# Expert results of a mixture-of-experts layer: added to the residual on chip by a one-hot product, instead of stored and gathered

## The reference, cut to what matters

```python
e_flat = (g_sel[:, None] * EXPERTS_PER_GROUP + top_i).reshape(-1)   # two of 32 experts per token
...
def run_block(args):
    xb, e = args
    return (jax.nn.silu(xb @ w_eg[e]) * (xb @ w_eu[e])) @ w_ed[e]
...
out = jnp.zeros((T, D_MODEL), jnp.float32).at[t_buf].add(y_buf.astype(jnp.float32) * w_buf[:, None])
```

## Time and profile before

| | us |
|---|---|
| median of 3 runs (lowest, highest) | 1305.26 (1303.16, 1308.2) |
| the profiled execution, its own time | 1295.43 |
| the profiled execution, span from first to last instruction | 1293.6 |
| PE busy, all of the span | 1077.7 (83%) |
| DVE, ACT, POOL busy | 427.6, 365.0, 195.6 |

### The profile page before, as it was taken

How to read it: one execution, slowest core, us unless ns; L and a number is a source line. 1 busy time by engine, 2 the same in 40 slices (tenths; PEclk the granted TensorE clock), 3 DMA queues, 4 the chain that set the end, 5 groups by cost and what they waited for, 6 DMA issues and landing times.

```text
span 1293.6 us, 15640 instructions
## 1 busy us (share of the span) xinstructions
PE 1077.7 (83%) x6419; PEld 764.3 (59%) x6419; DVE 427.6 (33%) x736; ACT 365.0 (28%) x567; POOL 195.6 (15%) x207
## 2 busy tenths in 40 slices
PE   4899799999999999999999378887877877877830
PEld 4898677777989899999999333222322322322310
DVE  5122667653256555434323511111111111101115
ACT  5313567565566443434211100000000000000002
POOL 7000110111313365513100000000000000000012
PEclk9999899999999999999989588898988988988975
DMA  7555222231222121252630789999999999999934
GB/s 198 187 104 109 64 50 46 45 51 39 67 65 65 51 74 58 74 155 72 189 140 33 284 355 419 428 427 427 427 428 429 426 427 431 427 427 429 400 117 155
DMA packets 101179, 284.67 MB, mean 220 GB/s; under 512 B 4588, under 2 KB 77512, under 8 KB 88824
## 3 DMA queue, kind: packets, MB, share of 16 engines
q1 hardware_dynamic: 91392, 256.39, 53.8%
q0 software_dynamic: 5936, 19.69, 4.1%
q10 hardware_dynamic: 3784, 7.65, 1.7%
HBM read 262.96 MB, written 20.75 MB: 219 GB/s over the span
## 4 chain that ended last, share of the span: by engine, by line
PE 55%; DMA 27%; DVE 8%; ACT 5%; issue 4%; POOL 1%; SPq 1%; POOLq 0%; ACTq 0%; DVEq 0%
DMA arena<-in_w_expert_up 23%; PE za L1020 12%; PE pj L713 10%; PE pj L714 10%; PE pj L715 10%; DMA ring<-in_w_in 2%; PE pj L740 2%; PE zb L1035 2%; DVE arena L1579 1%; DVE arena L1578 1%; PE zb L838 1%; DMA arena<-yd,arena 1%; PE ms L996 1%; ACT arena L1218 1%; PE zb L836 1%
## 5 line engine op out<-in xcount | busy, mean ns | idle before, releaser
L1020 PE MATMUL za<-arena 128*64 128x512 f32 x1024 | 246.4, 638 | 61.5 <-DMA arena<-in_w_expert_up 47.2
L713 PE MATMUL pj<-u_high_r,ring_r 128*128 128x288 f32 x768 | 236.9, 309 | 8.4 <-DVE ring_r L1462 4.8
L714 PE MATMUL pj<-u_rest_r,ring_r 128*128 128x288 f32 x768 | 227.8, 297 | 0.0
L715 PE MATMUL pj<-u_high_r,ring_r 128*128 128x288 f32 x768 | 227.7, 296 | 0.0
L1020 PEld LDWEIGHTS za<-arena 128*64 128x64 f32 x1024 | 81.0, 147 | 216.1 <-issue 148.2
L713 PEld LDWEIGHTS pj<-u_high_r,ring_r 128*128 128x128 f32 x768 | 145.8, 190 | 16.5 <-issue 11.2
L714 PEld LDWEIGHTS pj<-u_rest_r,ring_r 128*128 128x128 f32 x768 | 145.8, 190 | 2.2 <-issue 1.0
L715 PEld LDWEIGHTS pj<-u_high_r,ring_r 128*128 128x128 f32 x768 | 145.6, 190 | 0.0
L1035 PE MATMUL zb<-arena 128*64 128x512 f32 x512 | 124.9, 644 | 17.3 <-DVE arena L1910 15.1
L1462 DVE TENSOR_TENSOR ring_r<-ring,ring_r 128x1024 fp32r<-128x1024 f32 x68 | 85.6, 1266 | 120.7 <-ACT ring_r L1106 120.6
L1035 PEld LDWEIGHTS zb<-arena 128*64 128x64 f32 x512 | 40.1, 147 | 91.1 <-issue 73.3
(11 more groups left out here) (408 smaller groups left out, 1699.6 us busy)
## 6 DMA issues: line engine op xcount, KB each, us to landing
arena<-in_w_expert_gate SPq DMA_DIRECT2D x32, 2048.0 KB, 20.7
arena<-in_w_expert_up SPq DMA_DIRECT2D x32, 2048.0 KB, 19.4
arena<-in_w_expert_down SPq DMA_DIRECT2D x32, 2048.0 KB, 19.8
ring<-in_w_in SPq DMA_DIRECT2D x32, 512.0 KB, 8.2
ring<-in_w_gate SPq DMA_DIRECT2D x24, 512.0 KB, 4.1
yd<-arena SPq DMA_DIRECT2D x16, 512.0 KB, 22.0
yd<-arena POOLq DMA_DIRECT2D x1, 4608.0 KB, 18.8
arena<-in_x_prompt SPq DMA_DIRECT2D x8, 512.0 KB, 7.2
```

The costliest lines, as they stand in the source:

```text
L713: pe.matmul(out, left[0], right[0], start=k == 0, stop=False)
L714: pe.matmul(out, left[0], right[1], start=False, stop=False)
L715: return pe.matmul(out, left[1], right[0], start=False, stop=k == last - 1)
L1020: m = pe.matmul(za[j * BLK:(j + 1) * BLK, b, :], xT[:, k, j * BLK:(j + 1) * BLK], w[:, j * KD + k, :], start=k == 0, stop=k == KD - 1)
```

## The change

The results of a pair no longer leave the chip. For each pair, DVE builds `slot_hot` (128 rows by 640 tokens), which is 1 where row r belongs to token t. ACT and DVE take the two halves of the down product out of `zb`, multiply each row by its weight, and split it into a rounded part `y_high` and a remainder `y_rest`, both in the fp32r form that PE multiplies in one pass. PE multiplies `slot_hot` with both (`scatter`): 2 halves by 5 token tiles are 10 chunks of two matmuls with 512 columns, which go in turn through four PSUM banks (the two of `pj` and the two of `zb`), and DVE adds each chunk to `h` (`add`). The chunks of pair i-1 are spread over pair i: six behind the first transposes, two behind up, two behind the transposes of `hid`. Those of pair 15 come behind the loop and behind the nine `If`s.

Per-row weights need a second table product (`col_weight`, 20 more matmuls), and pair 0 now waits for it (`routed` at 3). The copy to `hidT` moves from DVE to ACT. `store_y`, `yd`, the zero fill, the final gathers and `experts_done` go. The overflow pairs get their own path (`scatter_over`, `add_over`) in the bodies of the `If`s.

```diff
@@ SP
-                    store_y(i)
...
-            sp.wait_ge(S["y_out"], 16 * EPAIRS)
...
-            sp.sem_inc(S["experts_done"], 1)
@@ PE
+            def scatter(i, parts, behind=True):
+                for k in parts:
+                    q, t = divmod(k, NT)
+                    o0, n = TT[t]
+                    if k == 0:
+                        pe.wait_ge(S["hot_r"], i + 1)
+                        if behind:
+                            pe.wait_ge(S["sc_r"], 2 * NT * i)
+                    if k == 3:
+                        pe.wait_ge(S["yl_r"], 2 * i + 2)
+                    pe.wait_ge(S["yl_r"], 2 * i + q + 1)
+                    if k >= NBANK:
+                        pe.wait_ge(S["sc_r"], 2 * NT * i + k - NBANK + 1)
+                    bank = add_bank(k)
+                    half = slice(q * 512, (q + 1) * 512)
+                    pe.matmul(bank[0:n, :], slot_hot[:, o0:o0 + n], y_high[:, half], start=True, stop=False)
+                    pe.matmul(bank[0:n, :], slot_hot[:, o0:o0 + n], y_rest[:, half], start=False, stop=True
+                              ).then_inc(S["sc_ps"], 1)
...
             def expert_pair(i, turn, before=True, over=None, first=False):
+                else:
+                    pe.wait_ge(S["routed"], 3)
...
                 m.then_inc(S["xt2_ps"], 1)
+                if mix:
+                    scatter(i - 1, range(6), not first)
                 pe.wait_ge(S["xt2_a"], i + 1)
...
+                if mix:
+                    scatter(i - 1, (6, 7))
                 pe.wait_ge(S["hid_r"], i + 1)
...
                 m.then_inc(S["hidt_ps"], 1)
+                if mix:
+                    scatter(i - 1, (8, 9))
+                    pe.wait_ge(S["sc_r"], 2 * NT * (i - 1) + 8)
                 pe.wait_ge(S["hidt_r"], i + 1)
...
                 with pe.If(total > j):
-                    expert_pair(EPAIRS + j, ((EPAIRS + j) % 2, (EPAIRS + j) // 2))
+                    expert_pair(EPAIRS + j, ((EPAIRS + j) % 2, (EPAIRS + j) // 2), over=j)
+                    scatter_over(j)
+            scatter(EPAIRS - 1, range(2 * NT))
@@ DVE
+                dve.tensor_tensor(col_weight, bc(iota_f[:, 0:NPC].unsqueeze(1), P, k2, NPC),
+                                  bc(flat[1].unsqueeze(2), P, k2, NPC), ALU.is_equal)
...
+                dve.wait_ge(S["route_ps"], 3)
+                dve.tensor_copy(slot_weight, ms[:, P:P + NPC]).then_inc(S["routed"], 1)
...
+            def add(i, parts, behind=True):
+                for k in parts:
+                    q, t = divmod(k, NT)
...
+                    v = h[0:n, t, q * 512:(q + 1) * 512]
+                    dve.tensor_tensor(v, v, add_bank(k)[0:n, :], ALU.add).then_inc(S["sc_r"], 1)
...
+                    dve.tensor_scalar(slot_hot, tok_no, slot_tok[:, bass.ds(i, 1)], None, ALU.is_equal)
...
+                        dve.scalar_tensor_tensor(out=y_rest[:, half], in0=zb[:, q, :],
+                                                 scalar=weight_now, in1=y_high[:, half],
+                                                 op0=ALU.mult, op1=ALU.subtract).then_inc(S["yl_r"], 1)
...
+            add(EPAIRS - 1, range(NT))
             for t in range(NT):
-                final(t)
+                add(EPAIRS - 1, (NT + t,))
                 if t > 0:
                     final_norm(t - 1)
@@ POOL
-            pool.dma_start(yd[NE * BLK:(NE + OVB) * BLK, :].rearrange("(c p) d -> p c d", p=P),
...
-            pool.wait_ge(S["experts_done"], 1)
...
-                    pool.indirect_dma_start(out=y_back[t % 2][s][0:n, :], out_offset=None, in_=yd,
```

More of the change, by code:

```diff
@@ L251 @@
 NEARLY = 3
+NBANK = 4
 NMIX = 2 + NT
@@ L434, in trunk_and_experts @@
         iota_pf = at(u2T_off + D + OVB * NE + P, P)
-        g_ffn = at(take(D), D)
+        g_ffn_off = take(D)
+        g_ffn = at(g_ffn_off, D)
         lg = at(take(NT * 36), NT, 36)
@@ L454, in trunk_and_experts @@
         eid = at(take(OVB), OVB)
+        take(-cut[0] % 8)
+        slot_hot = region("slot_hot", take(NT * P), NT * P)
+        tok_no = at(take(NT * P), NT * P).bitcast(I32)
         cut[0] = merged_off
@@ L461, in trunk_and_experts @@
         hid = at(take(DE), DE)
-        y_out_sb = at(take(D), D)
+        y_off = take(D)
         w_g = [at(wexp_off, 2 * KD, DE), at(take(2 * KD * DE), 2 * KD, DE)]
         assert cut[0] <= front
-        y_back = [[at(wexp_off + D * (2 * i + s), D) for s in range(2)] for i in range(2)]
+        y_high = region("y_high", y_off, D)
+        y_rest = region("y_rest", g_ffn_off, D)
+        over_high = region("over_high", u2_off, D)
+        over_rest = region("over_rest", u2_off + D, D)
+        over_hot = region("over_hot", u2T_off + D, NT * P)
+        square = [at(wexp_off + 16384 + D * i, D) for i in range(2)]
+        col_weight = at(merged_off + D + 2 * NT * P + 2 * NT * NPC, 2 * NT, NPC)
         cs = [small]
@@ L998, in ffn_turn, with scatter_over, expert_pair @@
                 m.then_inc(S["lg_ps"], 1)
-            def expert_pair(i, turn, before=True):
+            def scatter(i, parts, behind=True):
[16 more added lines that the diff above has]
+                              ).then_inc(S["sc_ps"], 1)
+            def scatter_over(j):
+                for k in range(2 * NT):
+                    t, q = divmod(k, 2)
+                    o0, n = TT[t]
+                    if k == 0:
+                        pe.wait_ge(S["hot_r"], EPAIRS + j + 1)
+                    pe.wait_ge(S["yl_r"], 2 * (EPAIRS + j) + q + 1)
+                    if k < 2:
+                        pe.wait_ge(S["sc_r"], 2 * NT * (EPAIRS - 1))
+                    else:
+                        pe.wait_ge(S["over_r"], 2 * NT * j + k - 1)
+                    half = slice(q * 512, (q + 1) * 512)
+                    pe.matmul(pj[0:n, q, :], over_hot[:, o0:o0 + n], over_high[:, half], start=True, stop=False)
+                    pe.matmul(pj[0:n, q, :], over_hot[:, o0:o0 + n], over_rest[:, half], start=False, stop=True
+                              ).then_inc(S["over_ps"], 1)
+                pe.wait_ge(S["over_r"], 2 * NT * (j + 1))
+            def expert_pair(i, turn, before=True, over=None, first=False):
+                mix = before and over is None
                 pe.wait_ge(S["xg_in"], (i + 1) * 16)
@@ L1027, in expert_pair @@
                 m.then_inc(S["hidt_ps"], 1)
+                if mix:
+                    scatter(i - 1, (8, 9))
+                    pe.wait_ge(S["sc_r"], 2 * NT * (i - 1) + 8)
                 pe.wait_ge(S["hidt_r"], i + 1)
                 pe.wait_ge(S["wd_in"], (i + 1) * 32)
-                for q, (done, free) in enumerate((("down_a", "y_a"), ("down_b", "y_b"))):
+                for q, done in enumerate(("down_a", "down_b")):
                     if before:
-                        pe.wait_ge(S[free], i)
+                        pe.wait_ge(S["yl_r"], 2 * i + q - 1)
                     for k in range(DE // P):
@@ L1054, in table @@
                 m.then_inc(S["route_ps"], 1)
+                pe.wait_ge(S["route_in"], 3)
+                for c in range(2 * NT):
+                    m = pe.matmul(ms[:, P:P + NPC], place_hot[:, c, :], col_weight[:, c, :], start=c == 0,
+                                  stop=c == 2 * NT - 1)
+                m.then_inc(S["route_ps"], 1)
             steps = {f.__name__: f for f in (past_keys, keys_out, dt_turn, att_scores, att_after, att_values,
@@ L1071, in _ @@
             expert_pair(0, (0, 0), before=False)
-            expert_pair(1, (1, 0))
+            expert_pair(1, (1, 0), first=True)
             with pe.Fori(1, EPAIRS // 2) as ii:
@@ L1360, in routing, with expert_pair @@
                 act.activation(for_exp, for_exp, ACT.Exp).then_inc(S["fexp_r"], 1)
-            def expert_pair(i, turn, before=True):
+            def expert_pair(i, turn, before=True, over=None):
                 act.wait_ge(S["xt2_ps"], i + 1)
@@ L1367, in expert_pair @@
                 act.activation(gate_t, za[:, 0, :], ACT.Tanh, scale=0.5).then_inc(S["gate_th"], 1)
[L1368 to L1372, removed]
+                act.wait_ge(S["hidt_ps"], i + 1)
+                act.activation(hidT, oa[:, :].rearrange("p (k l) -> p k l", k=4), ACT.Copy).then_inc(S["hidt_r"], 1)
+                for q, done in enumerate(("down_a", "down_b")):
+                    act.wait_ge(S[done], i + 1)
+                    if q == 0:
+                        act.wait_ge(S["hot_r"], i + 1)
+                    half = slice(q * 512, (q + 1) * 512)
+                    if over is None:
+                        if before and q == 0:
+                            act.wait_ge(S["sc_ps"], 2 * NT * i)
+                        act.activation(y_high[:, half], zb[:, q, :], ACT.Copy, scale=weight_now
+                                       ).then_inc(S["yh_r"], 1)
+                    else:
+                        if q == 0 and over == 0:
+                            for s in range(2):
+                                act.wait_ge(u2_out[s], 16 * ((NT + 1 - s) // 2))
```

(12 more changed lines are left out.)

85 lines of the change are left out of this document (53 added, 32 removed).

## The result

| | median, us | lowest, highest (runs) | profiled execution: own time, span |
|---|---|---|---|
| before | 1306.73 | 1303.16, 1309.69 (4) | 1295.43, 1293.6 |
| after | 1289.15 | 1288.46, 1290.2 (4) | 1289.0, 1287.1 |

The ratio is 0.9881, with a 95% interval from 0.9859 to 0.9902: 1.2% faster, a gain of 12.8 to 18.4 us on 1306.73, where 11.3 were forecast. The time lies in the range, 4.9 us under the forecast of 1294.0. (The kernel before has one run more here than in the first table.) All ratios are of fast runs alone: two executions of e7, of 1656.91 and 2721.63 us, were slow and are left out.

What follows compares the result with a forecast made beforehand. It took the pairs to be bound by DMA bytes; -15.9 + 2.5 + 2.6 - 0.5 = -11.3 us gave an own time of 1284.1, plus 9.8 a median of 1294.0, range 1284 to 1304 us.

Steps and rivals of the forecast that it cites:

- The loop: Pairs 0 to 12: 13 stores no longer sent, 1.22 us of DMA time each, -15.9 us.
- PE's chain: PE's work per pair in the loop: 28.0 us, 29.7 with one slow product, under the new period of 30.64.
- The end: From the last down product to the span's end: 50.3 us against 50.8, so -0.5.
- the walk: PE passing nine skipped overflow bodies before the last scatter: 26 us, starting 3.4 us ahead of the product's end.
- Rival A: At the end, passing the nine skipped bodies is cheap: -32.5 us in all, 1273; chance 0.07.
- Rival B: At the end, passing the larger skipped bodies costs more: +6 us or more, 1300 to 1304; chance 0.14.
- The start: Pair 0's transposes wait for the second table: +2.5 us, not covered, bounds 0 and +2.5.
- The zero fill: Its removal at the kernel's start: counted as nothing, bounds 0 and -3.6 us.
- The step that failed: Carrying the profiled execution's forecast own time, 1284.1 us, to the median by adding 9.8: 1294.0.
- +2.6 behind the last landing: Pairs 14 and 15, where PE sets the pace, pay the added chain: 0.3 and 2.3 us.

Runs made afterwards that it cites:

- e7: The changed kernel with the changes of e4 and e6 together; four of six executions took 1263.01 to 1268.5 us, ratio 0.971 to the kernel before.
- e3: The changed kernel with each pair's store put back, from y_high to a scratch tensor; 1306.11 us.
- e8: The changed kernel with two more products made and overwritten for each scatter chunk; 1319.38 us.
- e4: The changed kernel with one jump on PE around all nine overflow bodies; 1266.65 us.
- e5: The changed kernel with the nine Ifs on PE kept, each body a single wait, PE's overflow work left out; 1267.96 us.
- e6: The changed kernel with the second table's inputs formed ahead of the first table's result, its product in bank oa; 1287.56 us.
- e2: The changed kernel with the 4.6 MB zero fill and the waits for it put back; 1288.53 us.
- e1: Twelve more runs of the kernel before, unchanged; 1302.35 us, ratio 0.9988.
- e9: One more single profiled execution of the kernel before, unchanged; 1305.3 us.
- e10: Another single profiled execution of the kernel before, unchanged; 1305.23 us.

## Why the prediction came out as it did

**The loop** was right: 12 periods went from 382.34 to 367.92 us, -14.4 (1.22 a pair forecast, 14.7). e3 gives the bytes back, and the whole 14.5 with them. PE's chain, forecast at 28.0 us and 29.7 with a slow product, measures 27.3 by e8 and, from the landing at 854.74 with its product of 8.78 to the end of the next gate product, 29.5. The cover held, and e8 shows from where it no longer does.

**The end** was right in each part: what the gathers gave, the walk took, and e4 and e5 set 22.5 and 21.2 us of it free. Rival A had priced a walk that costs nothing at 21 us under the forecast, and falls with a walk of 25.6. Rival B falls: the bodies grew, the skips did not get dearer (25.6 us; the nine of before had a longest of 5.4, here it is 3.4, with the gathers gone).

**The start**: the second table makes the transposes 2.67 us later, as forecast, and it shows at the loop's first landing against the first profile as +0.6, where 2.5 less one store of 1.2, so +1.3, was forecast. e6 shows that little of it can be had back.

**The zero fill**: nothing that e2's time shows; its trace comes up below.

**The step that failed** is the one that carried the sum over to the median: the sum was made against the profiled execution, "the median shown, 1305.26, lies 9.8 above that own time; I take the same difference". After's own time is 1289.0 and its median 1289.15, so no such difference is left. Against the first profile the stages measure +5.7 in front of the tables, +0.6, -14.4, +2.0 and -0.4, together -6.5; forecast were 0, +1.3, -14.7, +2.6 and -0.5, so all stages behind the front are right to 0.7 us. But that execution of before was its best: the other three took 1.8 to 5.3 us more behind the last landing and 1.8 to 2.2 more up to the first. Against the mean of the four profiles of before (738.65, 81.29, 382.36, 45.86, 51.95) the stages measure +4.9, -0.9, -14.4, -1.1 and -1.4, -13.0 in sum (before rounding); the runs say 15.5 (1 - 0.9881 of 1306.73), as the four profiles, with own times of 1295.43 to 1305.3, still lie below before's median. So the term "+2.6 behind the last landing" had the right work and the wrong base: on an average execution the added chunks there cost less than the slow products that before's other three executions had. The runs of the changed kernel also seem to spread less: its four lie within 1.7 us and e2's six within 3.7, before's four within 6.5 and the 23 beside e1 within 11.8.

That the time still came within 4.9 us of the forecast is in part luck: the changed kernel's profiled execution came out 4.9 us above the forecast own time of 1284.1, for the most part by the front, which the sum had at nothing, and the 9.8 us added to it shrank to 0.15. The second miss went the other way and outweighed the first.

My first theory for the missing 4 us, a front that varies, fell with e1, e9 and e10, where the tables start between 737.8 and 740.2 us.

**What stays open.** In the eight profiles of changed code (after, e2 to e8) the tables start between 740.07 and 744.48, on average at 742.3, so 3.7 us later than in before's four, though little in front of them was changed. The delay arises in the first 160 us: the same small copy by ACT (L1169 of before, L1229 of after) starts at 155.99 to 158.66 us in before's four, at 160.47 to 162.60 in the seven without the fill, and at 159.01 in e2, which has it. So with the fill back, 1.8 us of an average delay of 4.4 are left at that point. That leans towards the missing fill as a part of the cause, but one profile doesn't show it. What makes an up product take 8.5 us or more is open too. Products of 8.5 us and more come mostly behind the longer waits, but not by their length: before's first profile has 9.75 us behind 4.75 and 8.65 behind 5.95, e3 has 7.09 behind 2.67, and e6 7.09 where after has 8.78. No run took the wait alone away.

## What to carry to other kernels

A loop that is bound by bytes gives back the time of the bytes that are taken from it (here 14.4 us of 14.7), as long as the engine that takes over the work stays under the new period: work out that chain first. Look at what an engine's queue must pass before the work that is moved to it: skipped bodies that nobody waited for became 22.9 us of the end, and one jump around all of them makes this kernel 1266.65 us, 2.9% faster than before instead of 1.2%. And sum a forecast against more than one profiled execution: a quick one hides a gain.

## What was not expected of the hardware

A skip in PE's queue costs 0.20 us when its target is at hand (e5) and 2.96 to 3.40 us when a page is fetched for it (after, eight fetches beside eight such skips); a jump over nine bodies took no longer, 3.36 us (e4). The same product of 32 matmuls takes 7.09 us at a granted clock of 1.00 and 8.78 at 0.81 (after), and the wait ahead of it doesn't settle which: 8.78 behind 2.49 us in after, 7.09 behind 2.48 in e6. In e9, behind an up product of 9.83, the two down products took 8.78 as well, though each had waited only 0.78.
